# Attention scores of two heads, in turns on the two row halves of TensorE

## What is computed

```
s_own = einsum('bhqd,bhkd->bhqk', q_c, k_own) * scale
s_own = where(causal, s_own, -inf)
p = softmax(s_all);  o = p @ v_own
```

```
s = einsum('bhqd,bhkd->bhqk', qb, kb) * scale
s = s + c[:, :, q0:k_end, None] - c[:, :, None, :k_end]
s = where(q_pos >= k_pos, s, -inf);  p = softmax(s);  o = p @ vb
```

## Time and profile before

| what | value |
|---|---|
| runs | 1274.25, 1266.86, 1266.7 us; median 1266.86 |
| profiled execution | 1265.16 us, its span 1263.4 us |
| PE busy | 1194.1 us, 95% of the span |
| DVE busy | 799.0 us, 63% |
| ACT busy | 592.2 us, 47% |
| granted TensorE clock, mean | 0.968 |
| attention "m" | about 60.7 to 149.4 us |
| attention "f" | about 634.1 us to 711 us |
| chain that ended last | PE 80%, DVE 10%, ACT 5% |

### The profile page before, as it was taken

One profiled execution on the slowest core, in us unless ns is written; L12 is line 12 of the kernel. 1 busy time (PEld: TensorE's weight loads), 2 busy tenths in 40 slices (PEclk: granted clock), 3 DMA queues, 4 the chain that ended last, 5 costly groups with the idle time before them and its releaser, 6 DMA issues.

```text
span 1263.4 us, 17533 instructions
## 1 busy us (share of the span) xinstructions
PE 1194.1 (95%) x7210; PEld 974.3 (77%) x7210; DVE 799.0 (63%) x1297; ACT 592.2 (47%) x905; POOL 121.3 (10%) x124
## 2 busy tenths in 40 slices
PE   7899799999999999999999999999988898999997
PEld 6767589797788888888867777887867776888785
DVE  5646664545866778554645688677776968555644
ACT  6465233223546556345544564454473336534531
POOL 0303141410000000000000000000321510000000
PEclk9998799999999999998989999999999799999999
DMA  8522111112455455553512265455533043655551
GB/s 292 177 100 84 34 50 54 48 34 100 154 183 181 174 183 176 183 183 119 168 51 99 100 237 180 153 194 187 187 126 122 4 159 125 208 190 183 189 192 55
DMA packets 49665, 177.45 MB, mean 140 GB/s; under 512 B 5648, under 2 KB 6288, under 8 KB 49328
## 3 DMA queue, kind: packets, MB, share of 16 engines
q1 hardware_dynamic: 49584, 176.32, 40.9%
HBM read 175.25 MB, written 1.05 MB: 140 GB/s over the span
## 4 chain that ended last, share of the span: by engine, by line
PE 80%; DVE 10%; ACT 5%; POOL 2%; issue 1%; DMA 1%; SPq 0%; DVEq 0%; ACTq 0%
PE wps L2583 20%; PE wps L2585 20%; PE wps L2584 20%; PE tps L2572 4%; DVE wlo L1757 2%; PE tps L2770 2%; PE tps L2629 2%; PE tps L2788 2%; PE tps L2779 1%; ACT whi L1384 1%; PE tps L2950 1%; PE tps L2882 1%; DVE arena L1982 1%; POOL arena L2476 1%; ACT over L1669 1%
## 5 line engine op out<-in xcount | busy, mean ns | idle before, releaser
L1757 DVE TENSOR_TENSOR wlo<-raw,whi 128x1024 fp32r<-128x1024 f32 (+1 forms) x322 | 388.6, 1231 | 197.0 <-ACT whi L1384 195.7
L2583 PE MATMUL wps<-whi,a_hi 128*128 128x512 f32 (+1 forms) x1008 | 407.2, 404 | 14.9 <-DVE a_lo L1779 8.4
L2585 PE MATMUL wps<-wlo,a_hi 128*128 128x512 f32 (+1 forms) x1008 | 396.4, 393 | 0.0
L2584 PE MATMUL wps<-whi,a_lo 128*128 128x512 f32 (+1 forms) x1008 | 396.2, 393 | 0.0
L1384 ACT ACTIVATE whi<-raw 128x1024 fp32r<-128x1024 f32 (+1 forms) x322 | 325.3, 1050 | 53.0 <-PE wps L2585 51.0
L2583 PEld LDWEIGHTS wps<-whi,a_hi 128*128 128x128 f32 x1008 | 193.4, 192 | 59.8 <-issue 11.1
L2585 PEld LDWEIGHTS wps<-wlo,a_hi 128*128 128x128 f32 x1008 | 192.3, 191 | 41.2
L2584 PEld LDWEIGHTS wps<-whi,a_lo 128*128 128x128 f32 x1008 | 193.4, 192 | 36.9
L2583 PE MATMUL wps<-whi,f_hi 128*128 128x512 f32 x264 | 104.6, 396 | 0.0
L2585 PE MATMUL wps<-wlo,f_hi 128*128 128x512 f32 x264 | 104.2, 395 | 0.0
L2584 PE MATMUL wps<-whi,f_lo 128*128 128x512 f32 x264 | 104.2, 395 | 0.0
(11 more groups left out here) (382 smaller groups left out, 1399.2 us busy)
## 6 DMA issues: line engine op xcount, KB each, us to landing
raw<-in_w_dn SPq DMA_DIRECT2D x22, 512.0 KB, 3.3
raw<-in_w_0dn SPq DMA_DIRECT2D x22, 512.0 KB, 3.3
raw<-in_w_1dn SPq DMA_DIRECT2D x22, 512.0 KB, 3.2
raw<-in_w_ua SPq DMA_DIRECT2D x20, 512.0 KB, 3.3
raw<-in_w_ub SPq DMA_DIRECT2D x20, 512.0 KB, 3.4
raw<-in_w_0ug SPq DMA_DIRECT2D x20, 512.0 KB, 3.3
raw<-in_w_0uu SPq DMA_DIRECT2D x20, 512.0 KB, 3.3
raw<-in_w_1ug SPq DMA_DIRECT2D x20, 512.0 KB, 3.3
```

The lines of the kernel that those rows point to most:

```text
L1757: V.tensor_tensor(t.wlo[n % NR][:, 0:w], t.raw[n % NR][:, 0:w], t.whi[n % NH][:, 0:w].bitcast(F32), ALU.subtract).then_inc(m.done(s.dve_lo ...
L2583: T.matmul(o, xh, wh, start=first, stop=False)
L2584: T.matmul(o, xl, wh, start=False, stop=False)
L2585: mm = T.matmul(o, xh, wl, start=False, stop=last)
```

## The change

Scores are now emitted once for each pair of heads, at even h, and what DVE and ACT do with them is a part of its own, `scored`, emitted for each head. In TensorE's part the four score products of the two heads stand together: query block 0 of the even head (lower row half), then of the odd head (upper row half), then block 1 of both. Behind them come, head by head, both forget products and both mask products. The mask product covers only the 128 columns on the diagonal in block 1, where it covered 256. Each head's end is signalled by its last mask product. There are four probability buffers and maxima in place of three.

```diff
@@ attention
-            if h_ < nh:
-                b = bank()
-                emit("scores", kind, h_, b.name, b.free, qk_t)
-                b.free = (("exp", kind, h_),)
+            if h_ < nh and h_ % 2 == 0:
+                bs = [bank(), bank()]
+                emit("scores", kind, h_ // 2, [b.name for b in bs], [b.free for b in bs], qk_t)
+                for u in range(2):
+                    emit("scored", kind, h_ + u, bs[u].name)
+                    bs[u].free = (("exp", kind, h_ + u),)
...
@@ place
-        t.mprob = [view(24, 384), view(25.5, 384), view(34, 384)]
+        t.mprob = [view(24, 384), view(25.5, 384), view(34, 384), sb("mprob3", [P, 384], F32, s1)[:, :]]
...
-        t.fprob = [sb(f"fprob{i}", [P, 384], F32, s4)[:, :] for i in range(3)]
+        t.fprob = [sb(f"fprob{i}", [P, 384], F32, s4)[:, :] for i in range(4)]
...
@@ scalar_program and vector_program (the rest of both parts is as before)
-    def scores(kind, h_, b, freed, ready):
+    def scored(kind, h_, b):
...
-        if h_ >= 3:
-            act.wait_ge(*m.at("probs_T", kind, h_ - 3))
+        if h_ >= 4:
+            act.wait_ge(*m.at("probs_T", kind, h_ - 4))
...
@@ tensor_program
     @part
-    def scores(kind, h_, b, freed, ready):
+    def scores(kind, i, banks, freed, ready):
+
         qT, kT = (t.mqT, t.mkT) if kind == "m" else (t.fqT, t.fkT)
-        p0, i = 64 * (h_ % 2), h_ // 2
         wait_all(ready)
-        wait_all(freed)
         pe.wait_ge(*m.at("tab"))
         for j in range(2):
-            nk = P * (j + 1)
-            o = t.bank[b][:, 0:P] if j == 0 else t.bank[b][:, P:3 * P]
-            T.matmul(o, qT[p0:p0 + 64, i, j * P:(j + 1) * P], kT[p0:p0 + 64, i, 0:nk], start=True, stop=False)
+            for u in range(2):
+                wait_all(freed[u])
+                r, nk = slice(64 * u, 64 * u + 64), P * (j + 1)
+                T.matmul(t.bank[banks[u]][:, P * j:P * j + nk], qT[r, i, j * P:(j + 1) * P], kT[r, i, 0:nk], start=j == 0, stop=False)
+        for u in range(2):
+            o, h_ = t.bank[banks[u]], 2 * i + u
             if kind == "f":
-                T.matmul(o, t.chead[0:96, h_:h_ + 1].to_broadcast([96, P]), t.cparts[0:96, 0:nk], start=False, stop=False)
-            mm = T.matmul(o, t.maskb[:, 0, :], t.maskb[:, 2 - j:3, :].rearrange("p a s -> p (a s)"), start=False, stop=True)
-        mm.then_inc(m.done(s.pe_side, "scores", kind, h_), 1)
+                for j in range(2):
+                    nk = P * (j + 1)
+                    T.matmul(o[:, P * j:P * j + nk], t.chead[0:96, h_:h_ + 1].to_broadcast([96, P]), t.cparts[0:96, 0:nk], start=False, stop=False)
+            T.matmul(o[:, 0:P], t.maskb[:, 0, :], t.maskb[:, 2, :], start=False, stop=False)
+            T.matmul(o[:, 2 * P:3 * P], t.maskb[:, 0, :], t.maskb[:, 2, :], start=False, stop=True).then_inc(
+                m.done(s.pe_side, "scores", kind, h_), 1)
```

More of the change, by code:

```diff
@@ L1171, in place @@
         t.fac = sb("fac", [P, 2, 4], F32, s1)
-        t.mmx, t.mnb = sb("mmx", [P, 3, 2], F32, s1), sb("mnb", [P, 3, 2], F32, s1)
+        t.mmx, t.mnb = sb("mmx", [P, 4, 2], F32, s1), sb("mnb", [P, 4, 2], F32, s1)
         t.msum = sb("msum", [P, 2, 8], F32, s1)
@@ L1203, in place @@
         t.frs = sb("frs", [P, 2, 16], F32, s4)
-        t.fmx, t.fnb = sb("fmx", [P, 3, 2], F32, s4), sb("fnb", [P, 3, 2], F32, s4)
+        t.fmx, t.fnb = sb("fmx", [P, 4, 2], F32, s4), sb("fnb", [P, 4, 2], F32, s4)
         t.fgq = sb("fgq", [P, 1], F32, s4)
@@ L1454, in scores @@
     @part
-    def scores(kind, h_, b, freed, ready):
-        nb, rs, prob = (t.mnb, t.msum, t.mprob[h_ % 3]) if kind == "m" else (t.fnb, t.frs, t.fprob[h_ % 3])
-        nb, rs = nb[:, h_ % 3, :], rs[:, :, h_]
+    def scored(kind, h_, b):
+        nb, rs, prob = (t.mnb, t.msum, t.mprob[h_ % 4]) if kind == "m" else (t.fnb, t.frs, t.fprob[h_ % 4])
+        nb, rs = nb[:, h_ % 4, :], rs[:, :, h_]
         act.wait_ge(*m.at("neg_max", kind, h_))
-        if h_ >= 3:
-            act.wait_ge(*m.at("probs_T", kind, h_ - 3))
+        if h_ >= 4:
+            act.wait_ge(*m.at("probs_T", kind, h_ - 4))
         activate(prob[:, 0:P], t.bank[b][:, 0:P], ACT.Exp, bias=nb[:, 0:1], accum_out=rs[:, 0:1]).then_inc(m.done(s.act_out, "exp_0", kind, h_), 1)
@@ L1852, in scores, with scored @@
     @part
-    def scores(kind, h_, b, freed, ready):
+    def scored(kind, h_, b):
         mx, nb, _, _, _ = softmax_tiles(kind)
-        mx, nb = mx[:, h_ % 3, :], nb[:, h_ % 3, :]
+        mx, nb = mx[:, h_ % 4, :], nb[:, h_ % 4, :]
         dve.wait_ge(*m.at("scores", kind, h_))
@@ L1862, in scores @@
             after_last()
-        if h_ >= 3:
-            dve.wait_ge(*m.at("probs_T", kind, h_ - 3))
+        if h_ >= 4:
+            dve.wait_ge(*m.at("probs_T", kind, h_ - 4))
         if kind == "f":
@@ L2619, in scores @@
     @part
-    def scores(kind, h_, b, freed, ready):
+    def scores(kind, i, banks, freed, ready):
         qT, kT = (t.mqT, t.mkT) if kind == "m" else (t.fqT, t.fkT)
-        p0, i = 64 * (h_ % 2), h_ // 2
         wait_all(ready)
-        wait_all(freed)
         pe.wait_ge(*m.at("tab"))
         for j in range(2):
-            nk = P * (j + 1)
-            o = t.bank[b][:, 0:P] if j == 0 else t.bank[b][:, P:3 * P]
-            T.matmul(o, qT[p0:p0 + 64, i, j * P:(j + 1) * P], kT[p0:p0 + 64, i, 0:nk], start=True, stop=False)
-            if kind == "f":
-                T.matmul(o, t.chead[0:96, h_:h_ + 1].to_broadcast([96, P]), t.cparts[0:96, 0:nk], start=False, stop=False)
-            mm = T.matmul(o, t.maskb[:, 0, :], t.maskb[:, 2 - j:3, :].rearrange("p a s -> p (a s)"), start=False, stop=True)
-        mm.then_inc(m.done(s.pe_side, "scores", kind, h_), 1)
+            for u in range(2):
[4 more added lines that the diff above has]
+            o, h_ = t.bank[banks[u]], 2 * i + u
+            if kind == "f":
+                for j in range(2):
[4 more added lines that the diff above has]
+                m.done(s.pe_side, "scores", kind, h_), 1)
     @part
     def probs_T(kind, g, b, freed):
-        prob = (t.mprob if kind == "m" else t.fprob)[g % 3]
+        prob = (t.mprob if kind == "m" else t.fprob)[g % 4]
         pe.wait_ge(*m.at("exp", kind, g))
```

## The result

The changed kernel takes 1261.09 us (median of 9 runs, 1258.69 to 1262.97) against 1266.7 of the kernel before in the same comparison. The ratio is 0.9949 with a 95% interval of 0.9928 to 0.9969: half a per cent faster, which the runs resolve, and less than the one per cent that I called a difference. The times of the kernel before fall into two groups: of its 65 executions in this and the later comparisons 42 took 1264.6 to 1268.6 us and 23 took 1273.8 to 1277.6, with a lower mean clock (0.957 to 0.963 against 0.964 to 0.970, where it is on record), and the share of the longer ones, 1 of 9 here and up to 9 of 17 later, moves a ratio by up to 0.4%. The profiled execution has a span of 1259.3 us against 1263.4, and a mean granted clock of 0.963 against 0.968.

The account below looks back on a forecast made before the run. PE was taken to set the pace of "f" and most of "m". 1265.16 - 2.0 ("f") - 3.3 ("m") = 1259.9 us for the profiled execution; allowing for the runs' median, 1260.5 was predicted, range 1251 to 1271.

Parts of the forecast that it names:

- "m": Attention "m": 3.3 us gained, 1.66 in each of the last two pairs; bounds 6.6 + 1.5 and -1.8.
- The scores on PE: Score, forget and mask products: a pair takes 1.52 us instead of 3.18, saving 1.66 a pair, 13.3 in "f".
- in turns: Score products alternating between row halves overlap: four of 256 columns take 1.07 us, a pair no more than one alone.
- The new waits in "f": In "f", DVE's queue puts two heads' maxima ahead of the copy PE needs: 10.3 us of new waits.
- The wait of 1.46 for L1889: PE's old wait before the transposes of head 4 in "f" goes, a gain of 1.5 us.
- The clock: In "f", new waits bring two falls to half clock in place of one, costing 2.5 us net.
- clock falls: Rival: new waits in "f" bring up to five clock falls, 3.2 us each, giving 1271.8 us; chance 0.22.
- "f" in sum: Attention "f" gains 4.5 us at full clock, less 2.5 for the clock: 2.0 us.
- The stage after: The stretch from the last value products of "f" to the first product of `drive`: no term was forecast.
- a later stage: Closing sign: the prediction is wrong if a stage behind gives the gained time back; no size given.
- the saving arrives: Rival: no clock fall in "f" and all of "m" counts, 14.3 us gained, 1251 us; chance 0.18.
- the halves don't overlap: Rival: score products on the two row halves run one after another, a pair costs 2.76 us, total 1271; chance 0.05.

Follow-up runs that it names:

- later_no_turns: values_later with TensorE's products made head by head as in the kernel before; 1251.91 us (ratio 0.9844).
- values_later: The change with both heads' value products one pair later, behind the scores of a later pair; 1244.97 us (ratio 0.9798).
- by_head: The change with both score products of the even head first, then both of the odd head; 1262.38 us, one run.
- kept_busy: The change with 9, 7 and 11 unused filler products ahead of the value products of heads 0, 2 and 4 of "f"; 1258.83 us (0.9905).
- pairs_exp_table: The change with one single-column exponential on ACT at the end of "f", to load its table there; 1258.2 us (0.9901).
- mask_256: The change with block 1's old 256-column mask product; 1258.84 us, one run.
- f_pairs_only: The change in attention "f" only; "m" keeps the old one-head-at-a-time part with the 256-column mask; 1265.12 us (0.996).
- m_pairs_only: The change in attention "m" only; "f" keeps the old one-head-at-a-time part, with four buffers; 1266.7 us (0.9969).
- copy_first: The change with the odd head's maxima and exponentials moved behind the copy of head h - 2, from the second pair on; 1264.41 us (0.9957).
- paired_no_turns: The change's list order, but PE's products as before: head by head, forget and mask behind each score product; 1272.85 us (1.001).
- later_exp_busy: values_later with a single-column exponential after "f" and 2, 3, 3 filler products in waits at the start of "f"; 1239.45 us (0.9757).

## Why the prediction was right, and where it was not

The sum came out, 1260.5 against 1261.09, with terms that were off in both directions. That it fits so closely is luck: "f" gained 3.9 us more than predicted, "m" 0.9 less, and 4.2 us were lost where the prediction had nothing.

- **The scores on PE.** Right to the hundredth by rows: 1.53 us a pair against 1.52, 0.86 for the four products. The saving is 1.66 a pair between `later_no_turns` and `values_later`, as predicted, 13.3 in eight; the two estimates from the lengths of "f" give 12.0 and 11.9. But "in turns" was not the reason (`by_head`).
- **The new waits in "f".** The mechanism, the heads named and the order of DVE's queue were right. The size was not: 8.6 us of waits for the copy and the exponentials against 10.3. I had 2.5 at the start (measured 1.99), 1.5 (1.21), 2.5 (2.18), 1.9 and 1.9 (1.55 and 1.55). The wait of 1.46 for L1889 went, as predicted.
- **The clock.** I had put two falls in place of one, 2.5 us net. There were three in place of two (the one at 701.66 I had left out), but each 3.41 us long, and the sum at half clock stayed at 10.2 us. The net is nothing. The rival "clock falls" had a fall at each of the five waits; three brought one. It was wrong on the price, which it took from one row. `kept_busy` gives 1.6 us for each fall of 3.41, half of the 3.2 that the prediction took, since these falls were half as long as the one of 6.83.
- **"f" in sum:** 5.9 us gained where I had 2.0: 12.0 (by the lengths of "f") - 6.2 - 0 in place of 13.3 - 8.8 - 2.5.
- **"m":** 2.4 us where I had 3.3, with a spread of about 1 between kernels that do the same there. The longer wait at head 0, by 2.4, is as predicted.
- **The stage after.** The step that failed: I had written nothing for what follows "f", and it cost 2.8 us, of which only the closing words on "a later stage" give a hint. The runs showed in its place a table load of 1.28 us that moved in front of the weights' path, 1.4 us, and a fall of the clock behind the longer wait, 1.4 (`pairs_exp_table`, `mask_256`). I had listed what every engine must do and its order, but not the table that ACT holds between its functions. The 0.9 us after that, and 0.5 before and between the attentions, were not followed up; the trace of the change has one more stretch of 3.41 us at 0.50 there, at 1061.52.
- **The rival "the saving arrives"** (1251) fell with the waits, and "the halves don't overlap" with the first pair's rows.

Behind the prediction, these expectations missed: `by_head` in the time of a pair; `f_pairs_only` and `m_pairs_only` by 1.8 and 2.4 us; `copy_first` by 2.4; `paired_no_turns` by 3; `values_later` by 9, in "m"; `later_no_turns`, 6 us under its range and above its rival's; `later_exp_busy` by 0.6.

What stays open: why the clock is at 0.50 for 20.5 us in "f" in two kernels that have the old products there, with no wait ahead of the stretch in either and PE never idle within it in one of them; and why `later_no_turns`, with the same products, has none.

## What to carry to other kernels

When an engine is relieved, first ask how far apart the list puts a result and its use: here the later use with the old products was worth 1.6%, the faster products in the change's order 0.5%, and the two together 2% (1.2, 0.4 and 1.8% against the shorter executions of the kernel before). When an operation is moved past another on ACT, look for the table each of them needs, since a load of 1.28 us can move from a place where nobody waits for it to the chain. Small idle stretches on TensorE can have a second price in the clock, 1.6 us for each fall here, which cheap filler products can take away where a wait can't be.

## What the runs showed of the hardware

Products of 64 rows on opposite row halves overlap without being written in turns: 0.86 us for four products in both orders. Waits of 1.2 to 2.2 us were each followed by 3.41 us at 0.50 in "f" of the change at heads 0, 2 and 4, and those of 1.55 at heads 8 and 12 by none; in `kept_busy` the one at head 8 was. Four waits of 0.25 to 0.44 us within 3 us were followed by 6.83 us at 0.50 (`values_later`); with fillers in three of them no fall came (`later_exp_busy`). And the clock can stay at 0.50 for 20.5 us under a PE that is never idle (`m_pairs_only`), which goes with an "f" 7.6 us longer than before in code whose products the experiment had not touched.
